# Gated-delta gates as token rows: a, b and two heads' z in one weight stream, outputs gated on rows and turned by VectorE and GpSimd

## What is computed

```python
h = rms_norm(x, norm_w)
proj = jnp.einsum('btd,de->bte', h, w_in)     # rq,rk,rv,rg, gqkv,gz,ga,gb, mq,mk,mv,mz
qkv = jax.nn.silu(causal_depthwise_conv(gqkv, conv_w))          # 6 gated-delta heads
beta = jax.nn.sigmoid(gb)
g = -jnp.exp(a_log) * jax.nn.softplus(ga + dt_bias)
o_gdn = gated_delta_rule(gq, gk, gv, g, beta)
y_gdn = from_heads(rms_norm(o_gdn, gdn_norm_w)) * jax.nn.silu(gz)
y = jnp.concatenate([y_ret, y_gdn, y_moba], axis=-1)
return x + jnp.einsum('bte,ed->btd', y, w_out)
```

## Time and profile before

| what | value |
|---|---|
| median of 3 runs | 517.66 us (517.51 to 517.90) |
| the profiled execution | 517.88 us |
| its span in the trace | 515.5 us |
| PE busy / PEld busy | 509.4 us (99%) / 427.4 us (83%) |
| DVE / ACT / POOL busy | 338.8 us (66%) / 278.9 us (54%) / 128.4 us (25%) |
| DMA | 91.68 MB, 178 GB/s in the mean |

### The profile page before, as it was taken

The page is one execution under the profiler, slowest core; times in us unless marked ns, Lnnn a source line. Parts: engine busy times, 40 slices in busy tenths (PEclk is TensorE's granted clock), DMA queues, the critical chain, the costliest instruction groups (busy, mean ns, idle before and its releaser), DMA issues.

```text
span 515.5 us, 8854 instructions
## 1 busy us (share of the span) xinstructions
PE 509.4 (99%) x3464; PEld 427.4 (83%) x3464; DVE 338.8 (66%) x520; ACT 278.9 (54%) x457; POOL 128.4 (25%) x164
## 2 busy tenths in 40 slices
PE   8999999999999999999999999999999999999997
PEld 5888888888888888888888888888888888888885
DVE  3999999989776876555654555655467555646451
ACT  4776655755357676564545554664556456343340
POOL 4764243415131312110510050105010510230000
PEclk9999999999999999999999999999999999999999
DMA  8999646665745465575676477657765557757711
GB/s 273 314 292 236 182 123 164 176 174 147 202 118 132 125 162 153 135 200 155 174 187 183 124 204 206 170 159 199 186 183 164 167 161 225 214 187 221 257 41 41
DMA packets 146923, 91.68 MB, mean 178 GB/s; under 512 B 7907, under 2 KB 135874, under 8 KB 146882
## 3 DMA queue, kind: packets, MB, share of 16 engines
q1 hardware_dynamic: 143392, 88.94, 62.6%
q10 hardware_dynamic: 3490, 2.18, 1.5%
HBM read 89.00 MB, written 2.10 MB: 177 GB/s over the span
## 4 chain that ended last, share of the span: by engine, by line
PE 96%; DMA 1%; SPq 1%; ACT 0%; issue 0%; DVE 0%; DVEq 0%
PE pj L1484 20%; PE pj L1487 20%; PE pj L1486 20%; PE pj L1462 14%; PE pj L1463 7%; PE pj L1532 2%; DMA w_raw<-in_w_in_dram 1%; PE pj L1541 1%; PE mx L1629 1%; PE pj L1459 1%; PE mx L1682 1%; PE mx L1664 1%; PE mx L1740 1%; PE mx L1809 1%; PE pj L1458 0%; SPq L400 0%
## 5 line engine op out<-in xcount | busy, mean ns | idle before, releaser
L357 DVE TENSOR_TENSOR w_lo<-w_raw,w_hi 128x1024 fp32r<-128x1024 f32 x160 | 200.2, 1259 | 86.5 <-ACT w_hi L455 86.0
L455 ACT ACTIVATE w_hi<-w_raw 128x1024 fp32r<-128x1024 f32 x159 | 167.4, 1057 | 124.9 <-PE pj L1487 105.2
L1484 PE MATMUL pj<-w_hi,hT 128*128 128x512 f32 x320 | 127.0, 397 | 0.0
L1486 PE MATMUL pj<-w_hi,hT 128*128 128x512 f32 x320 | 125.9, 393 | 0.0
L1487 PE MATMUL pj<-w_lo,hT 128*128 128x512 f32 x320 | 124.9, 390 | 0.0
L1462 PE MATMUL pj<-hT,w_hi 128*128 128x512 f32 x300 | 109.6, 405 | 0.0
L1463 PE MATMUL pj<-hT,w_lo 128*128 128x256 f32 x300 | 84.0, 280 | 0.0
L1487 PEld LDWEIGHTS pj<-w_lo,hT 128*128 128x128 f32 x320 | 60.1, 188 | 12.4
L1484 PEld LDWEIGHTS pj<-w_hi,hT 128*128 128x128 f32 x320 | 60.1, 188 | 11.9
L1486 PEld LDWEIGHTS pj<-w_hi,hT 128*128 128x128 f32 x320 | 60.2, 188 | 11.4
L1462 PEld LDWEIGHTS pj<-hT,w_hi 128*128 128x128 f32 x300 | 56.3, 188 | 14.0 <-DVE w_lo L357 1.4
(11 more groups left out here) (240 smaller groups left out, 518.0 us busy)
## 6 DMA issues: line engine op xcount, KB each, us to landing
w_raw<-in_w_in_dram SPq DMA_DIRECT2D x256, 256.0 KB, 3.4
w_raw<-in_w_out_dram SPq DMA_DIRECT2D x64, 256.0 KB, 3.9
big<-in_x_dram SPq DMA_DIRECT2D x9, 256.0 KB, 5.2
out_dram<-sq ACTq DMA_DIRECT2D x7, 256.0 KB, 5.7
big<-in_x_dram SPq DMA_DIRECT2D x3, 512.0 KB, 7.4
cst<-table_dram SPq DMA_DIRECT2D x1, 682.0 KB, 9.5
big<-in_x_dram SPq DMA_DIRECT2D x2, 128.0 KB, 2.8
out_dram<-sq ACTq DMA_DIRECT2D x1, 128.0 KB, 2.5
```

What stands on the lines that cost most here:

```text
L357: eng.tensor_tensor(w_lo[:, n % NSPLIT, :], w_raw[:, n % NRAW, :], w_hi[:, n % NSPLIT, :].bitcast(F32), ALU.subtract).then_inc(S("lo"), 1)
L455: act.activation(w_hi[:, n % NSPLIT, :], w_raw[:, n % NRAW, :], ACT.Copy).then_inc(S("hi_done"), 1)
L1484: ins = pe.matmul(bank[:, :], src[:, kc, 0, tok], hi[:, k, :], start=first, stop=False)
L1486: pe.matmul(bank[:, :], src[:, kc, 1, tok], hi[:, k, :], start=False, stop=False)
```

## The change

The gated-delta weights get a new order of tiles: 8 tiles for the first group as before; 4 tiles (unit 64 to 96) that hold the z columns of the last two heads with the a and b columns, 268 columns by 4 K blocks (`AB_K`, `SLOT`); 28 tiles (to unit 320) for the other 14 sections of q, k and v; 8 tiles (to unit 384) for the z columns of the first four heads, in the form of the head groups. So all z, a and b have tokens on the partitions. `wab`, `whole`, `ab_products`, `K_SUM`, the product at `U_SUM` and `out_transposes` go, with `gated_pair` and `split_y`. ScalarE evacuates the new parts with `evacuate_ab` and `evacuate_gates`, VectorE has one small instruction more (`half`) ahead of the low part of tile 8, the gated-delta outputs are gated in `norm_out` and turned by `turn_rows`, `spread_rows` and `split_rows`. The points of the decay and solve stages lie 9 units later.

```diff
-U_SUM, U_CUM = 71, 118
-U_ROWS = (130, 166, 228)
-U_PREP = (144, 198, 262)
-U_SOLVE = 290
+U_CUM = 127
+U_ROWS = (139, 175, 237)
+U_PREP = (153, 207, 271)
+U_SOLVE = 299
...
+            def evacuate_ab(c):
+                act.wait_ge(S("half"), 1)
+                bank = mx[(0, 3)[c]]
+                z = bank[:, 0:2 * P].rearrange("p (h e) -> p h e", h=2)
+                act.activation(ab[:, A_Z, c, :], bank[:, 2 * P:2 * P + GDN], ACT.Copy, scale=sm[:, 6 + c:7 + c])
+                act.activation(ab[:, A_TB, c, :], bank[:, 2 * P + GDN:AB_COLS], ACT.Tanh, scale=sm[:, 60 + c:61 + c])
+                act.activation(chunk_of(th3[:, :, 2], c), z, ACT.Tanh, scale=sm[:, 60 + c:61 + c])
+                act.activation(chunk_of(gate_of(2), c), z, ACT.Copy, scale=sm[:, 6 + c:7 + c]).then_inc(S("ev_done"), 1)
+            def evacuate_gates(c):
+                act.wait_ge(S("silu_kq"), 2 * GDN)
+                z = pj[2 + c][:, :].rearrange("p (a h e) -> p a h e", a=2, h=2)
+                act.activation(th3[:, :, 0:2, c * P:(c + 1) * P], z, ACT.Tanh, scale=sm[:, 60 + c:61 + c])
+                for a in range(2):
+                    ins = act.activation(chunk_of(gate_of(a), c), z[:, a], ACT.Copy, scale=sm[:, 6 + c:7 + c])
+                ins.then_inc(S("ev_done"), 1)
...
-            for n in range(KC):
-                ...
-                pool.wait_ge(S("h_lo"), n + 1)
-                pool.tensor_tensor(whole(n), hT[:, n, 0, :].bitcast(F32), hT[:, n, 1, :].bitcast(F32), ALU.add).then_inc(S("h_whole"), 1)
...
             dve.tensor_copy(rb[:, :], mx[1][:, 0:T]).then_inc(S("rb_done"), 1)
+            dve.wait_ge(S("rstd_done"), 1)
+            dve.tensor_scalar(sm[:, 60:62], sm[:, 6:8], 0.5, None, ALU.mult).then_inc(S("half"), 1)
             advance(50)
...
-            dve.wait_ge(S("abt_psum"), 1)
-            dve.tensor_tensor(abT, mx[0][:, 0:T], rb[:, :], ALU.mult).then_inc(S("abt_done"), 1)
...
             conv(0, 0, 0)
-            advance(69)
+            advance(77)
+            conv(0, 1, 0)
+            advance(86)
             dve.wait_ge(S("bias_in"), 2 * 16)
-            dve.wait_ge(S("tanh_b"), 1)
+            dve.wait_ge(S("ev_done"), EV_AB + 2)
             ...
-            advance(77)
-            conv(0, 1, 0)
-            advance(82)
+            conv(0, 0, 1)
+            advance(93)
             dve.wait_ge(S("exp_z"), 1)
...
+                elif g < GDN and kind == "ab":
+                    hi, lo = (w[:, n % NSPLIT, :].rearrange("p (k c) -> p k c", k=AB_K) for w in (w_hi, w_lo))
+                    k, c = r // 2, r % 2
+                    kc = i * AB_K + k
+                    first, last = kc == 0, kc == KC - 1
+                    bank = mx[(0, 3)[c]][:, 0:AB_COLS]
+                    tok = slice(c * P, (c + 1) * P)
+                    pe.matmul(bank, hT[:, kc, 0, tok], hi[:, k, :], start=first, stop=False)
+                    pe.matmul(bank, hT[:, kc, 1, tok], hi[:, k, :], start=False, stop=False)
+                    ins = pe.matmul(bank, hT[:, kc, 0, tok], lo[:, k, :], start=False, stop=last)
...
-            ab_products().then_inc(S("abt_psum"), 1)
-            stream(U_SUM)
-            pe.wait_ge(S("abt_done"), 1)
-            for c in range(C):
-                ins = pe.matmul(mx[1][:, c * AB:(c + 1) * AB], abT[:, c * P:(c + 1) * P], cst[:, K_SUM:K_SUM + AB], start=True, stop=True)
...
-            def out_transposes(p, bank):
-                pe.wait_ge(S("on"), p + 1)
-                for n in range(4):
-                    ins = pe.transpose(bank[:, n * P:(n + 1) * P], on[:, n // 2, n % 2, :], ident)
-                ins.then_inc(S("otr"), 1)
...
+                    turn_rows(p - 1)
...
+            def split_gdn(p):
+                split_rows(p, Y_BLOCK["gdn"] + 2 * p, [sm[:, 96 + RET:97 + RET]])
```

More of the change, by code:

```diff
@@ L292, in feat, with part, used_cols, block_of @@
             return x[:, (2 * h + c) * P:(2 * h + c + 1) * P]
[L294 to L306, removed]
+        def part(t):
+            for kind, at in (("gate", T_GATE), ("feat", T_FEAT), ("ab", T_AB), ("first", 0)):
+                if t >= at:
+                    return kind, t - at
+        def used_cols(t):
+            return slice(0, SLOT if T_AB <= t < T_FEAT else TK * 512)
+        def block_of(tile, at):
             return tile[:, at:at + P]
@@ L1450, in unit @@
                     wait_lo(pe, n)
-                if g < GDN:
-                    s, kc = place(t, r)
+                kind, i = part(t)
+                if g < GDN and kind == "feat":
+                    m, kc = 4 + i // 2, i % 2 * UPT + r
+                    bank = pj[m % 4]
                     first, last = kc == 0, kc == KC - 1
                     if first:
-                        pe.wait_ge(S("ev_done"), 4 * (g - 1) + s + 1)
-                    high, low = (block_of(w[:, n % NSPLIT, :], g, s, r) for w in (w_hi, w_lo))
+                        pe.wait_ge(S("ev_done"), feat_ev(m - 4) + 1)
+                    high, low = (block_of(w[:, n % NSPLIT, :], r * P) for w in (w_hi, w_lo))
@@ L1461, in unit @@
                     else:
-                        pe.matmul(pj[s][:, :], high, hT[:, kc].rearrange("p a t -> p (a t)"), start=first, stop=False)
-                        ins = pe.matmul(pj[s][:, 0:T], low, hT[:, kc, 0, :], start=False, stop=False)
-                else:
-                    hi = w_hi[:, n % NSPLIT, :].rearrange("p (k c) -> p k c", k=TK)
-                    lo = w_lo[:, n % NSPLIT, :].rearrange("p (k c) -> p k c", k=TK)
+                        pe.matmul(bank[:, :], high, hT[:, kc].rearrange("p a t -> p (a t)"), start=first, stop=False)
@@ new lines, in unit @@
+                        ins = pe.matmul(bank[:, 0:T], low, hT[:, kc, 0, :], start=False, stop=False)
+                elif g < GDN and kind == "ab":
+                    hi, lo = (w[:, n % NSPLIT, :].rearrange("p (k c) -> p k c", k=AB_K) for w in (w_hi, w_lo))
[7 more added lines that the diff above has]
+                    ins = pe.matmul(bank, hT[:, kc, 0, tok], lo[:, k, :], start=False, stop=last)
+                    if last:
+                        ins.then_inc(S("proj_done"), 1)
+                else:
+                    hi = w_hi[:, n % NSPLIT, 0:TK * 512].rearrange("p (k c) -> p k c", k=TK)
+                    lo = w_lo[:, n % NSPLIT, 0:TK * 512].rearrange("p (k c) -> p k c", k=TK)
@@ L1540, in first_group_low @@
                     last = t == TPH - 1 and k == TK - 1
[L1541 removed]
+                    ins = pe.matmul(pj[s][:, 0:T], block_of(lo, k * 512 + s * P), hT[:, TK * t + k, 0, :], start=False, stop=last)
                     if last:
```

467 lines of the change are left out of this document (226 added, 241 removed).

## The result

The changed kernel takes 524.04 us in the median (523.89 to 525.70), against 517.68 (517.51 to 517.90) for the kernel before beside it: a ratio of 1.0125, interval 1.0112 to 1.0137. It is 6.4 us slower, where 514.5 was forecast and 517.8 was the top of the range.

The account below looks back on a forecast made before the run. TensorE was taken as the bound, with VectorE a second bound from 60 to 114 us. Work -3.5, waits +0.5 and start -0.3 sum to -3.3 us on 517.88, so 514.5 us, with 8 in 10 from 513.3 to 517.8.

Parts of the forecast that it names:

- What leaves TensorE, and what the new order costs: TensorE's work: a and b products, U_SUM product and output transposes go, 268-column matmuls at 0.124 each come; net -3.5 us.
- R2: Rival: the 268-column matmuls are bound by their weight loads, up to +6.3 us, so 520.8; chance 5%.
- Eight token tiles 21.76, 2.72 each: Pace of token-major tiles on TensorE, against 2.80 taken for feature tiles; eight gate tiles give back 0.6 us.
- Waits (1): Tile 8: TensorE waits for VectorE's low part, behind the copy of the norms and `half`; +0.75 us.
- (2): Tile 9: its low part is ready at 38.0, while TensorE wants it at 37.7; +0.35 us.
- (3): Gate chain: VectorE idles 2 us for ScalarE's evacuations, making tile 15's low part late for TensorE; +0.1 us.
- (4): `decay_sums` stands behind another low part and a convolution, ending near 63.0 when TensorE wants it at 62.7; +0.3 us.
- R1: Rival: VectorE's waits spend the gain, through long convolutions and low parts (+2.5) and no start gain (+0.3): 517.3; chance 15%.
- (5): Past unit 144: the 9-unit shift gives VectorE's steps 3.2 us more room, so earlier small waits go; -1.0 us.
- I take nothing: Output gating and turning moved off TensorE to VectorE, ScalarE and GpSimd costs TensorE nothing; without cover up to 0.5 us.
- R3: Rival: turned outputs or gates come late in three chain stages, stalling TensorE 1 to 2 us each: 519.0; chance 3%.
- The start: Start of the kernel: GpSimd's 16 adds go, so VectorE's low part there is faster; -0.3 us, bounds 0 and -0.6.

Follow-up runs that it names:

- a_all: a_align with U_PREP one unit earlier, a_gate's three VectorE moves, and the second pair's low split behind the next stage's copy of k: 514.79 us, ratio 0.9933.
- b_yt64: The kernel before with 64 unused bytes ahead of yT, putting yT at the weights' place modulo 256 bytes: 517.34 us, ratio 0.9985.
- a_align: The changed kernel with w_hi and w_lo pitch at 1088 floats instead of 1072 and 128 unused bytes ahead of yT: 519.32 us, ratio 1.0024.
- a_prep: a_align with the three prepare stages one unit earlier (U_PREP 152, 206, 270 instead of 153, 207, 271): 518.30 us, ratio 1.0005.
- a_gate: a_align with three VectorE moves: tile 8's low part and conv(0, 0, 1) earlier, decay_sums back where it stood before the change: 516.49 us, ratio 0.9969.

## Why the prediction was wrong, step by step

**What leaves TensorE, and what the new order costs: right.** The 268-column matmuls are the first point of the forecast, 0.124 us from start to start. TensorE in order of time at tile 8:

```profile
33.24 0.24 PE L1634 MATMUL mx<-cst,prow 95*128 95x95 f32 x1
34.24 0.39 PE L1514 MATMUL mx<-w_hi,hT 128*128 128x268 f32 x1 [0.76 <-DVE w_lo L382]
34.47 0.28 PE L1515 MATMUL mx<-w_hi,hT 128*128 128x268 f32 x1
34.59 0.28 PE L1516 MATMUL mx<-w_lo,hT 128*128 128x268 f32 x1
```

34.47 to 34.59 is 0.12. The four tiles take 34.24 to 46.23, 11.99 us for 96 matmuls, against 11.9 in the sum. R2 (bound by loads) is refuted: at a load's own length of 0.188 these tiles would have cost over 6 us more. With it falls, in this case, the sentence of the Trainium skill that a load overlaps a running matmul only when its row group differs (TensorE: Matmul & The Clock Gate, "The mechanism" of its part on packing). The same section also has loads to a background weight buffer pulled ahead of running matmuls; 0.124 us a matmul agrees with that. The transposes and the products of a and b are gone. The sum of -3.5 wasn't measured alone. The best witness for it is `a_all`: 3.3 under the kernel before, of which `b_yt64` puts 0.7 down to the address of `yT`; and it has 1.7 us of waits outside the start that the kernel before hasn't. That leaves -4.3 for the work and the small waits that went, where the forecast has -3.5 and -1.0. From the parameters' transpose to the end the two traces differ by 2.6 and not 3.3, which would leave -3.6: the two terms hold to about 1 us, no closer.

**"Eight token tiles 21.76, 2.72 each": the step that failed.** I took the pace of a token tile from the trace of before as a property of the instruction. It is one of the instruction and of where its operands lie, and the diff moved them: `SLOT` stood in it, I costed it as "the same columns in longer pieces" for the loads, and asked of no other reader of those buffers what a new pitch does to it. The same trace had the sign of it: beside the eight head tiles in 21.76 stand eight output tiles in 21.98 (467.58, above), for the same twelve matmuls, a window that I didn't take. A difference of 1% between equal instructions was a question that I didn't ask. In place of 2.72 the changed kernel's dense tiles took 2.74 to 2.80, going round with the buffers. Price: 4.7 us by `a_align`, of a miss of 9.5; 0.7 of the 4.7 is what the kernel before paid as well.

**Waits (1), tile 8: right.** +0.75 forecast, 0.76 measured, on VectorE's low part. **(2), tile 9:** +0.35 forecast, not seen, as VectorE began the low parts of tiles 9 and 10 at 35.84 and not at 36.4; it appeared at 0.22 as soon as `a_gate` made TensorE earlier.

**(3), the gate chain: the mechanism right, the size off.** VectorE in order of time, from its wait for ScalarE:

```profile
48.75 0.17 DVE L1067 TENSOR_TENSOR ab<-ab,bias 128x12 f32<-128x12 f32 x1 [2.37 <-ACT big L531]
...
54.42 1.22 DVE L382 TENSOR_TENSOR w_lo<-w_raw,w_hi 128x1024 fp32r<-128x1024 f32 x1
```

Idle 2.37 (2 forecast), start 48.75 (48.7), and the low part of tile 15 ends at 55.6 (55.6). But TensorE wanted it at 54.9 and not at 55.5: I had put unit 96 at 47.0, with the wait at tile 9, and it was 46.23. So the wait was 0.7 instead of 0.1. From 48.7 on VectorE's side was worked out to 0.1 us, TensorE's was not; where two engines meet, what is early on one is a wait, not a gain.

**(4), `decay_sums`: mis-sized.** +0.3 forecast, 0.42 idle and 0.58 by the starts. It ended at 63.7, 0.7 later than I had it, since the convolution ahead of it took the long form, beside GpSimd's adds of a section (60.15 to 62.39):

```profile
60.83 2.37 DVE L1044 SCALAR_TENSOR_TENSOR big<-raw,pcol,big 128x256 f32<-128x256 f32 x3
```

I had argued that GpSimd is silent between units 64 and 112. It wasn't wholly: it added the first four sections from 35.89 to 41.19, and the convolution at 38.76 took 2.72. The one at 60.83 comes behind that stretch. R1 had the right durations here in a smaller part.

**(5), "past unit 144 the small waits go": wrong.** A shift of 9 units isn't 3.2 us of room for everything. A list of stages that waits for sections and tiles of 16 and 8 units has edges, and two of the three prepare stages (207 + 2 past 208, 271 + 2 past 272) were pushed over one. The first cost 0.85 at tile 28, as `a_prep` shows. The wait of 0.90 at the last prepare stage isn't explained by the edge: it grew when the stage was put ahead of it. What TensorE waits for there is VectorE's SiLU at 117.18 (changed kernel), behind the low part at 113.88 and a convolution of 2.23 us at 115.02; nothing was run to take it away, and the cause stays open. The -1.0 of this step became +1.8 in these two waits.

**"I take nothing" for the moved outputs:** 0.53 us in the first retention stage, of the kind that R3 names, but once, where R3 had three stages at 1 to 2 us each. I had looked at GpSimd's copies and at `rms_power`, not at VectorE's split that waits for ScalarE's. No wait of TensorE ends with the GpSimd copies, as forecast.

**The start:** -0.3 forecast; the parameters' transpose starts at 33.24 against 33.69. In the traces of the experiments it starts anywhere from 32.99 to 34.87, so I don't count it.

In one sum, forecast to result: of the miss of 9.5 us, 4.7 are addresses (`a_align` against the changed kernel) and 4.5 the order of VectorE and ScalarE (`a_all` against `a_align`). The last 0.3 is where `a_all` lies over the forecast; in it a better address of `yT` (-0.7) and more leftover waits (1.7 for my net 0.5) nearly cancel. The interval failed too: its upper end was made of waits alone, and no rival had slower head and output tiles (R2 was about the 268-column matmuls).

## What to carry to other kernels

When a diff changes the size of any SBUF buffer, list the start addresses of every TensorE operand modulo 256 bytes before and after; a matmul's pace read from the old trace holds only where the distances stay. For token-major matmuls as here, pad buffer pitches to a multiple of 256 bytes, and put stationary and moving operands at the same offset; an unused 64 bytes won 0.7 us in the kernel before, and 128 bytes in the wrong place cost it 6. When hand-placed stages are shifted, check each against the edges of tiles and sections, not against the mean distance.

## What the runs showed of the hardware

- The pace of 512-column float32r matmuls depends on the distance between stationary and moving operand in SBUF, modulo 256 bytes: 2.72 us for twelve at 0 (2.74 with the changed kernel's pitch), 2.75 at 192, 2.79 at 128, 2.80 at 64. It was seen with token blocks stationary and weight columns moving. What in the chip does it was not shown, nor whether it holds for other sizes and types.
- Loads of 128x128 in a stream of 268-column matmuls overlap the matmuls and each other: 0.124 us from matmul to matmul (0.119 with 256 columns), with loads that last 188 ns.
- Three convolution instructions of VectorE take 1.52 us (97.55) or 2.37 (60.83); the two lengths stood in the kernel before too, and here the long one ran beside GpSimd's adds (60.15 to 62.39), the short one had none beside it.
